# Gathered expert rows in four chains of three half-row cells, and four more mixing-weight units kept on chip

## The chip, the cores and the metric

The kernel runs on one core of one Trainium2 chip. The metric is the device time of one execution, in microseconds (us).

## What is computed

One layer of a hybrid decoder for 1024 prompt tokens and 8 sample tokens, all in float32, D = 1024 channels. A trunk (state-space branch, gated recurrent branch, mixing of the two, output projection) comes first. Behind it stands the expert retrieval, which moves most of the bytes:

```python
q = (xc @ w_q).reshape(PEER_BLOCK, PEER_HEADS, 2, PEER_DK)
...
eidx = jnp.take_along_axis(cidx.reshape(...), sel, axis=-1)      # 8 heads x 16 experts of 16384 for each token
g = jax.nn.softmax(cs, axis=-1)
u = u_tab[eidx]
act = jax.nn.gelu(jnp.einsum('chkd,cd->chk', u, xc).astype(jnp.float32))
w = (g * act).astype(xc.dtype)
return jnp.einsum('chk,chkd->cd', w, v_tab[eidx])
```

So every token needs 128 rows of u (4 KB each) for dot products with its own vector, and the same 128 rows of v (4 KB each), weighted and added. The mixing that the change touches as well is `sigmoid(g_a) * (a_out @ w_proj_a) + sigmoid(g_b) * (b_out @ w_proj_b)`.

## The kernel before

**Chunks and slots.** The prompt is worked on in four chunks (c = 0 to 3) of 256 tokens, two tiles of 128. An expert slot is one expert of each of the 128 tokens of a tile. A chunk has 256 slots, there are 1024 in all and 8 more for the sample tokens. For each slot GpSimd issues one indirect DMA, the gather: it takes 128 rows of the table `uv`, whose rows hold u and v side by side (8 KB), one into each partition, 1 MB together.

**The path of a slot.** The gather lands in one of UV = 8 places of `uvring` (u in the first half of a place, v in the second), in turn. Slot number `at` uses place `at % UV`. VectorE multiplies u by the tokens' vectors and sums (the dot, in `dots`, which signals `u_used`). Two slots make a batch (PAIR = 2): ScalarE turns the two dots into weights (`weigh`) and spreads each on a diagonal `dg`; TensorE multiplies `dg` by v and adds in PSUM (`values`, which signals `v_pe`). A place is free again when TensorE has read v: that is what `gather_to` waits for, eight gathers back. GpSimd does its gathers in order and does nothing else.

**The trunk between the batches.** The trunk of chunk c + 1 is interleaved with the batches of chunk c by hand-written positions (`upto(...)` on each engine): VectorE does the scans, the mixing gates and the top-16 lists in between dots; TensorE the projections in between `values`.

**Weights.** SyncE loads trunk weights through a ring of two 8 KB slots; a pair of units (1 MB for the mixing weights `w_ab`, four pairs) is loaded when the pair two before it has been used. Some units are RESIDENT: loaded once in chunk 0 and kept for chunks 1 to 3. In chunk 0 the eight units of `w_ab` lie in places of the gather ring (from `MIX_AT`) that the first gathers don't need yet, and gathers 4 to 7 wait for the mixing products of chunk 0 (`unit`) before they overwrite them.

Of the kernel before, what the change touches and what calls it, by code (L numbers as in the profile page):

```python
# [14 lines left out]
P = 128  # L15
# [38 lines left out]
UV = 8  # L54
# [26 lines left out]
            ("w_out", 6), ("w_out", 7))  # L81
PARKED = (("w_out", 0),)
GLU_W = tuple(("w_glu", m) for m in range(4))
HOMES = RESIDENT + PARKED + GLU_W + tuple(MIX_W)
# [197 lines left out]

def dve_slots(c, i):

    return max(SLOT * c + i, 0) - pe_slots(c, i)
# [71 lines left out]
def build(nc, i_, o_):  # L357

    with ExitStack() as ctx:
# [6 lines left out]
        def sem(name):  # L366
# [94 lines left out]
        assert W.at <= T.at + UV * 2 * D  # L461
# [3 lines left out]
        uvring = R.take(UV, 2 * D)  # L465
        hn = [R.take(D) for _ in range(2)]
        acc = [R.take(D) for _ in range(2)]
        rows_ = uvring.rearrange("p a b -> p (a b)")
        GLU_AT, MIX_AT = 6 * D, 8 * D
        assert W.at <= T.at + GLU_AT and MIX_AT + KT * D <= UV * 2 * D  # L470
        homes = [R.take(D) for _ in RESIDENT] + [acc[1]] \
            + [rows_[:, GLU_AT + DB * k:GLU_AT + DB * k + DB] for k in range(QT)] \
            + [rows_[:, MIX_AT + D * k:MIX_AT + D * k + D] for k in (LAST_FIRST.index(m) for m in range(KT))]
# [268 lines left out]
        def _(pool):  # L742
# [62 lines left out]
        def _(act):  # L805
# [126 lines left out]
            def first_lists(upto):  # L932
# [42 lines left out]
                square_sum(0, 0, P, uvring[:, 0, 0:D])  # L975
# [232 lines left out]
        def _(dve):  # L1208
# [467 lines left out]
            def last_row():  # L1676
# [3 lines left out]
                return stt(acc[1], uvring[:, place(c, i) % UV, D:2 * D], wt[:, (BC - 1) % DOTS, PAIR - 1:PAIR], acc[1])  # L1680
# [30 lines left out]
            def dots(c, b):  # L1711

                for k in range(PAIR):
# [3 lines left out]
                    u = uvring[:, at % UV, 0:D]  # L1717
# [3 lines left out]
            def row(c, b):  # L1721

                i = PAIR * b + PAIR - 1
                if on_dve(SLOT * c + i) and (c, b) != (CH - 1, BC - 1):
# [3 lines left out]
                    stt(acc[t], uvring[:, place(c, i) % UV, D:2 * D], wt[:, b % DOTS, PAIR - 1:PAIR], acc[t]).then_inc(v_dve, 1)  # L1728
# [42 lines left out]
            def sample():  # L1771

                dve.wait_ge(hnS_in, 16 * NS)
                for h in range(HEADS):
                    at = sample_place(h)
                    dve.wait_ge(uv_in[at % UV], 16 * (at // UV + 1))
                    u = uvring[:, at % UV, 0:D]
# [227 lines left out]
        def _(pe):  # L2005
# [122 lines left out]
            def values(c, b):  # L2128
# [4 lines left out]
                for k in range(PAIR):  # L2133
                    i = PAIR * b + k
                    if not on_dve(SLOT * c + i):
                        last = i - i % (SLOT // 2) + SLOT // 2
                        for half in range(2):
                            at = D + 512 * half
                            for r, o in zip((0, HP), TURNED[half]):
                                ins = mm(PV[o:o + HP, half], dg[r:r + HP, PAIR * (b % 2) + k],  # L2140
                                         uvring[r:r + HP, place(c, i) % UV, at:at + 512],
# [22 lines left out]
            def sample():  # L2164

                for h in range(HEADS):
                    pe.wait_ge(w8_ok, h + 1)
                    for half in range(2):
                        at = D + 512 * half
                        ins = mm(PS[0:NS, half], w8[:, h], uvring[:, sample_place(h) % UV, at:at + 512],  # L2170
# [380 lines left out]
```

## Time and profile before

| what | us |
|---|---|
| median of 3 runs | 3084.43 |
| lowest and highest run | 3083.14, 3085.8 |
| span of the profiled execution | 3084.7 |

The profile gives the execution's span, from its first to its last instruction, and no other time for it; it lies 0.3 us from the median of the runs. In the profile PE is TensorE's matmuls, PEld its weight loads, DVE VectorE, ACT ScalarE, POOL GpSimd, SP SyncE. A line such as L759 is that of a helper, so that one line stands for all gathers (L759), all dots of prompt slots (L1718), all `values` matmuls (L2140), all mixing matmuls (L2184).

### The profile page before, as it was taken

Reading aid. Unit: us, or ns where it says so; the run is one execution under the profiler, and the core shown is the slowest. Engines: PE = TensorE matmul, PEld = TensorE weight load, DVE = VectorE, ACT = ScalarE, POOL = GpSimd, SP = SyncE. Lnnn points to the kernel's source line nnn. Section 1 sums busy time; section 2 is a strip of 40 time slices with the busy share of each in tenths; the row PEclk is TensorE's granted clock in tenths of the full one; section 3 lists DMA queues with packets and bytes.
Section 4 is the critical chain, followed back from the end, with each engine's and each line's share of the span. In section 5 each row is a group of like instructions: output and inputs, shape, how many; then the busy total and the mean of one; then the engine's idle time right before and its main releaser. Section 6 shows DMA issues by size and latency. Waiting matters only on the chain.

```text
span 3084.7 us, 40759 instructions
## 1 busy us (share of the span) xinstructions
PE 2367.6 (77%) x14560; PEld 1190.1 (39%) x14560; DVE 2150.7 (70%) x5361; ACT 1001.2 (32%) x3275; POOL 1202.5 (39%) x1048
## 2 busy tenths in 40 slices
PE   9997769888876778789777678888987676555565
PEld 7864325555343334455233324444433331111111
DVE  7758887765579887665468887766558897544445
ACT  2224332422334332432234332432233443222223
POOL 0013343443344443343343443434344444444442
PEclk9999889999999989989988879999998886777777
DMA  4569999999999999999999999999999999999997
GB/s 154 208 244 398 420 421 420 415 414 399 420 420 418 420 420 419 418 392 420 420 419 417 421 420 408 420 394 420 418 420 420 420 416 419 416 406 420 420 419 328
DMA packets 177898, 1226.32 MB, mean 398 GB/s; under 512 B 22664, under 2 KB 23048, under 8 KB 32160
## 3 DMA queue, kind: packets, MB, share of 16 engines
q0 software_dynamic: 148608, 1082.20, 84.9%
q1 hardware_dynamic: 27440, 136.67, 11.2%
q10 hardware_dynamic: 1648, 4.85, 0.4%
q8 instruction: 115, 1.88, 0.3%
q14 instruction: 87, 0.71, 0.1%
HBM read 1219.09 MB, written 4.55 MB: 397 GB/s over the span
## 4 chain that ended last, share of the span: by engine, by line
DMA 45%; PE 26%; DVE 15%; ACT 5%; POOL 3%; issue 3%; ACTq 1%; DVEq 0%; SPq 0%; POOLq 0%
DMA arena<-in_uv,arena 44%; PE psum L2140 11%; DVE arena L1718 7%; PE psum L2037 7%; ACT arena L807 4%; POOL arena L759 3%; PE psum L2184 3%; DVE arena L1212 3%; PE psum L2204 2%; DVE arena L1220 1%; DMA arena<-in_w_ab 1%; PE psum L2216 1%; ACT L807 1%; ACTq L831 1%; DVE arena L1590 1%
## 5 line engine op out<-in xcount | busy, mean ns | idle before, releaser
L759 POOL DMA_INDIRECT arena<-in_uv,arena x1032 | 1199.3, 1162 | 1856.2 <-PE psum L2140 1525.3
L1718 DVE CUSTOM_DVE_ANT_0 arena<-arena 128x1024 f32<-128x1024 f32 x1024 | 1246.8, 1225 | 789.4 <-DMA arena<-in_uv,arena 781.5
L2140 PE MATMUL psum<-arena 64*64 64x512 f32 x8184 | 1226.7, 723 | 669.9 <-ACT arena L807 622.5
L807 ACT ACTIVATE arena<-arena 128x1 f32<-128x1 f32 (+4 forms) x2746 | 727.1, 302 | 1850.8 <-DVE arena L1718 1741.9
L2140 PEld LDWEIGHTS psum<-arena 64*64 64x64 f32 x8184 | 301.2, 151 | 1401.1 <-ACT arena L807 923.5
L2037 PE MATMUL psum<-arena 128*128 128x256 f32 (+1 forms) x2656 | 632.4, 393 | 7.7 <-ACT arena L807 6.9
L2037 PEld LDWEIGHTS psum<-arena 128*128 128x128 f32 x2656 | 504.3, 194 | 193.6 <-issue 121.8
L1212 DVE TENSOR_TENSOR arena<-arena 128x256 f32<-128x256 f32 (+12 forms) x561 | 249.9, 472 | 12.1 <-issue 0.4
L807 ACT ACT_TABLE_LOAD x119 | 152.7, 1283 | 11.2 <-DVE arena L1212 7.1
L807 ACT ACTIVATE arena<-psum 128x256 f32<-128x256 f32 (+5 forms) x254 | 98.3, 402 | 144.9 <-PE psum L2037 94.4
L2184 PE MATMUL psum<-arena 128*128 128x128 f32 (+2 forms) x640 | 123.6, 351 | 9.5 <-DMA arena<-in_w_ab 7.2
L2184 PEld LDWEIGHTS psum<-arena 128*128 128x128 f32 x640 | 103.2, 196 | 37.2 <-issue 19.4
L1220 DVE SCALAR_TENSOR_TENSOR arena<-arena 128x256 f32<-128x256 f32 (+8 forms) x287 | 99.0, 357 | 19.3 <-ACT arena L807 13.9
L2204 PE MATMUL psum<-arena 128*128 128x512 f32 x192 | 90.3, 614 | 0.0
L1718 DVE DVE_READ_ACCUMULATOR2_ANT arena<- 128x1 f32 x1024 | 83.6, 82 | 0.0
L1486 DVE TENSOR_TENSOR_SCAN arena<-arena 128x64 f32<-128x64 f32 x256 | 68.9, 331 | 1.3
L1220 DVE SCALAR_TENSOR_TENSOR arena<-arena,psum 128x128 f32<-128x128 f32 (+4 forms) x97 | 46.0, 513 | 33.6 <-PE psum L2184 28.9
L2216 PE MATMUL psum<-arena 128*128 128x256 f32 (+1 forms) x320 | 63.2, 354 | 0.4 <-issue 0.4
L1212 DVE TENSOR_TENSOR arena<-psum,arena 128x512 f32<-128x512 f32 (+2 forms) x91 | 59.6, 684 | 2.8 <-PE psum L2140 1.8
L2216 PEld LDWEIGHTS psum<-arena 128*128 128x128 f32 x320 | 52.6, 200 | 22.5 <-issue 17.8
L2204 PEld LDWEIGHTS psum<-arena 128*128 128x128 f32 x192 | 35.2, 193 | 56.3 <-issue 56.3
L2052 PEld LDWEIGHTS psum<-arena 32*128 32x128 f32 x512 | 35.0, 207 | 28.9 <-issue 26.2
(134 smaller groups left out, 981.9 us busy)
## 6 DMA issues: line engine op xcount, KB each, us to landing
arena<-in_w_in SPq DMA_DIRECT2D x56, 1024.0 KB, 9.0
arena<-in_w_q SPq DMA_DIRECT2D x34, 1024.0 KB, 9.4
arena<-in_uv,arena POOLq DMA_INDIRECT x1032, 13.7
arena<-in_w_ab SPq DMA_DIRECT2D x12, 1024.0 KB, 9.4
arena<-in_w_out SPq DMA_DIRECT2D x11, 512.0 KB, 15.8
arena<-in_keys SPq DMA_DIRECT2D x17, 256.0 KB, 8.3
arena<-in_w_ab SPq DMA_DIRECT2D x8, 512.0 KB, 10.8
arena<-in_x_tok SPq DMA_DIRECT2D x8, 512.0 KB
```

Source lines behind the costliest of these rows:

```text
L759: pool.indirect_dma_start(uvring[:, r], None, i_["uv"], bass.IndirectOffsetOnAxis(column, 0)).then_inc(uv_in[r], 16)
L807: return nc.scalar.activation(out, in_, f, **kw)
L1212: return V.tensor_tensor(out, a, b, op)
L1220: return V.scalar_tensor_tensor(out=out, in0=a, scalar=s1, in1=b, op0=op0, op1=op1)
L1486: return V.tensor_tensor_scan(v, mag2[:, j:j + 1].to_broadcast([P, SEG]), v, start, ALU.mult, ALU.add)
L1718: V.tensor_tensor_reduce(out=u, in0=u, in1=hn[i // (SLOT // 2)], scale=1.0, scalar=0.0, op0=ALU.mult, op1=ALU.add, accum_out=dots_[:, b % ...
L2037: ins = mm(PB[u % 2][:, 0:n], w[:, P * t:P * t + P], rhs[:, t, 0:n], start=(t == 0), stop=(t == k - 1))
L2052: ins = mm(SB[j % 2][:, 2 * SEG * part:2 * SEG * part + 2 * SEG], wT[o:o + 32, QT * (2 * r + part) + q], uS[o:o + 32, q, 2 * SEG * r:2 * S ...
L2140: ins = mm(PV[o:o + HP, half], dg[r:r + HP, PAIR * (b % 2) + k], uvring[r:r + HP, place(c, i) % UV, at:at + 512], start=(i % (SLOT // 2) = ...
L2184: ins = mm(banks[side][:, 0:cols.stop - cols.start], w[:, 512 * side + P * t:512 * side + P * t + P], src[:, t, cols], start=(t == 0), sto ...
L2204: ins = mm(OUTB[t][half][0:rn], hT[c][:, k, r0:r0 + rn], w[:, 512 * half:512 * half + 512], start=(k == 0), stop=(k == KT - 1))
L2216: ins = mm(PB[s][:, 0:n], w[:, P * t:P * t + P], gb[:, t, cols], start=(t == 0), stop=(t == KT - 1))
```

## The change

A place now has three 4 KB cells for two slots' worth of turns. There are four chains of three cells; slot `at` belongs to chain `at % 4`. Its u always lands in the middle cell. Its v lands in the left cell on even turns and in the right cell on odd ones, so that u and v are still one 8 KB run in each partition: for the left side a second table `vu` (v first, then u) is gathered. The ring needs 12 cells of 4 KB where it had 8 places of 8 KB. The 16 KB per partition that this frees hold four more units of `w_ab` (2 to 5) for good, so that chunks 1 to 3 load two pairs of `w_ab` where they loaded four. A gather now also waits until the dot of the slot four before it has read the middle cell.

```diff
-UV = 8
+CHAINS = 4
+CELLS = 3 * CHAINS
+UV = 2 * CHAINS
...
 RESIDENT = (("w_out", 1), ("w_out", 2), ("w_out", 3), ("w_out", 4), ("w_out", 5),
-            ("w_out", 6), ("w_out", 7))
+            ("w_out", 6), ("w_out", 7), ("w_ab", 2), ("w_ab", 3), ("w_ab", 4), ("w_ab", 5))
...
-HOMES = RESIDENT + PARKED + GLU_W + tuple(MIX_W)
+MIX_PARKED = tuple(("w_ab", m) for m in LAST_FIRST[0:4])
+MIX_CELLS = (9, 10, 8, 11)
+HOMES = RESIDENT + PARKED + GLU_W + MIX_PARKED
...
+def u_cell(at):
+
+    return 3 * (at % CHAINS) + 1
+
+
+def v_cell(at):
+
+    return 3 * (at % CHAINS) + (2 if at // CHAINS % 2 else 0)
...
-            def gather(r, column):
-                pool.indirect_dma_start(uvring[:, r], None, i_["uv"],
-                                        bass.IndirectOffsetOnAxis(column, 0)).then_inc(uv_in[r], 16)
+            def gather(at, column):
+                first = D * min(u_cell(at), v_cell(at))
+                table = i_["vu"] if v_cell(at) < u_cell(at) else i_["uv"]
+                pool.indirect_dma_start(rows_[:, first:first + 2 * D], None, table,
+                                        bass.IndirectOffsetOnAxis(column, 0)).then_inc(uv_in[at % UV], 16)
 
             def gather_to(at, column):
 
+                before = at - CHAINS
+                if sample_place(0) <= before < sample_place(HEADS):
+                    pool.wait_ge(us_used, before - sample_place(0) + 1)
+                elif before >= 0:
+                    pool.wait_ge(u_used, before - (HEADS if before >= sample_place(HEADS) else 0) + 1)
                 before = at - UV
...
-                gather(at % UV, column)
+                gather(at, column)
...
-                    if c == 0 and i * 2 * D == GLU_AT:
-                        pool.wait_ge(glu_mm, 2 * QT)
-                    if c == 0 and MIX_AT <= i * 2 * D < MIX_AT + KT * D:
-                        m = 2 * i - MIX_AT // D
-                        pool.wait_ge(unit, U_MIX1 + m + 2)
+                    if c == 0 and i < UV:
+                        held = {u_cell(i), v_cell(i)}
+                        if held & {GLU_AT // D, GLU_AT // D + 1}:
+                            pool.wait_ge(glu_mm, 2 * QT)
+                        if held & set(MIX_CELLS):
+                            pool.wait_ge(unit, U_MIX1 + 1 + max(k for k, cell in enumerate(MIX_CELLS) if cell in held))
```

VectorE, TensorE and ScalarE run the same instructions as before, on other addresses.

GpSimd's queue at the start of chunk 0 was this before (`unit` counts finished products of trunk weights, `glu_mm` those of the gate):

```order
L759 DMA arena<-in_uv,arena 128x2048 [waits best_ok]
L759 DMA arena<-in_uv,arena 128x2048 x2
L759 DMA arena<-in_uv,arena 128x2048 [waits glu_mm]
L759 DMA arena<-in_uv,arena 128x2048 [waits unit] x4
L759 DMA arena<-in_uv,arena 128x2048 [waits v_pe,idx_ok]
L759 DMA arena<-in_uv,arena 128x2048 [waits v_pe] x7
```

It is this now:

```order
L775 DMA arena<-in_vu,arena 128x2048 [waits best_ok]
L775 DMA arena<-in_vu,arena 128x2048
L775 DMA arena<-in_vu,arena 128x2048 [waits glu_mm]
L775 DMA arena<-in_vu,arena 128x2048 [waits unit]
L775 DMA arena<-in_uv,arena 128x2048 [waits u_used] x2
L775 DMA arena<-in_uv,arena 128x2048 [waits u_used,unit,glu_mm]
L775 DMA arena<-in_uv,arena 128x2048 [waits u_used,unit]
L775 DMA arena<-in_vu,arena 128x2048 [waits v_pe,u_used,idx_ok]
L775 DMA arena<-in_vu,arena 128x2048 [waits v_pe,u_used] x3
```

From the fifth gather on every gather also waits for a dot (`u_used`), here and to the end of the program.

SyncE's queue at the mixing of chunk 1 was this before:

```order
L634 DMA arena<-in_w_glu 128x1024 [waits unit] x2
L634 DMA arena<-in_w_ab 128x2048 [waits unit] x4
L634 DMA arena<-in_w_out 128x1024 [waits unit]
L661 DMA arena<-in_x_tok 128x1024 [waits y_out0,lru_ok]
L662 DMA arena<-in_x_tok 128x1024
```

It is this now:

```order
L648 DMA arena<-in_w_glu 128x1024 [waits unit] x2
L648 DMA arena<-in_w_ab 128x2048 [waits unit] x2
L648 DMA arena<-in_w_out 128x1024 [waits unit]
L675 DMA arena<-in_x_tok 128x1024 [waits y_out0,lru_ok]
L676 DMA arena<-in_x_tok 128x1024
```

Two loads of 1 MB are gone, and what stands behind them moves up by two turns of the ring. Chunks 2 and 3 read the same.

## Rows read from the trace of the kernel before

**Rows 1.** The page: busy time of the engines, and the 40 slices

```profile
PE 2367.6 (77%) x14560; PEld 1190.1 (39%) x14560; DVE 2150.7 (70%) x5361; ACT 1001.2 (32%) x3275; POOL 1202.5 (39%) x1048
...
DMA  4569999999999999999999999999999999999997
GB/s 154 208 244 398 420 421 420 415 414 399 420 420 418 420 420 419 418 392 420 420 419 417 421 420 408 420 394 420 418 420 420 420 416 419 416 406 420 420 419 328
```

**Rows 2.** The page: the chain that ended last, by engine

```profile
DMA 45%; PE 26%; DVE 15%; ACT 5%; POOL 3%; issue 3%; ACTq 1%; DVEq 0%; SPq 0%; POOLq 0%
```

**Rows 3.** The page's costliest groups: the gather (L759) and the dot (L1718)

```profile
L759 POOL DMA_INDIRECT arena<-in_uv,arena x1032 | 1199.3, 1162 | 1856.2 <-PE psum L2140 1525.3
L1718 DVE CUSTOM_DVE_ANT_0 arena<-arena 128x1024 f32<-128x1024 f32 x1024 | 1246.8, 1225 | 789.4 <-DMA arena<-in_uv,arena 781.5
```

**Rows 4.** Waits: who waited for whom; us in total, times, longest us

```profile
POOL arena L759 <- PE psum L2140: 1525.3, 592, 10.9
...
DVE arena L1718 <- DMA arena<-in_uv,arena: 781.5, 581, 5.2
```

**Rows 5.** Timeline of VectorE: start us, us, instruction, idle before it

```profile
2708.45 1.23 DVE L1718 CUSTOM_DVE_ANT_0 arena<-arena 128x1024 f32<-128x1024 f32 x1 [1.26 <-DMA arena<-in_uv,arena]
...
2710.93 1.23 DVE L1718 CUSTOM_DVE_ANT_0 arena<-arena 128x1024 f32<-128x1024 f32 x1 [1.25 <-DMA arena<-in_uv,arena]
```

**Rows 6.** The gather's line alone: ns min/median/max, and us to landing

```profile
L759 POOL DMA_INDIRECT arena<-in_uv,arena x1032: 932/940/2665, 188.7 to 3057.9; - x172
...
DMA to landing us min/median/max: 5.5/13.7/21.8
```

**Rows 7.** The same view of the one gather issued at 749.0

```profile
DMA to landing us min/median/max: 6.8/6.8/6.8
```

**Rows 8.** The page's DMA issues: mixing weights; count, KB each, us to landing

```profile
arena<-in_w_ab SPq DMA_DIRECT2D x12, 1024.0 KB, 9.4
```

**Rows 9.** Windows over mixing stages; last three numbers: clock, DMA share, GB/s

```profile
736.00:746.00 10.00, 10.00 (x61) 7.62 (x60) 2.83 (x8) 0.95 (x4) 1.87 (x2) 0.99 1.02 392
746.00:762.00 16.00, 16.00 (x95) 9.88 (x94) 13.19 (x25) 3.82 (x15) 7.27 (x5) 1.00 0.91 339
...
1411.00:1460.00 49.00, 47.09 (x272) 30.35 (x271) 26.98 (x53) 10.49 (x40) 17.37 (x16) 0.97 1.01 420
2138.00:2185.00 47.00, 44.06 (x261) 27.27 (x260) 27.32 (x57) 10.25 (x38) 15.67 (x15) 1.00 1.01 421
```

**Rows 10.** The chain at the mixing of chunk 1: start us, us, what

```profile
719.53 10.69 DMA arena<-in_w_ab
...
740.78 6.91 PE psum L2184 x32
...
778.83 18.11 DMA arena<-in_uv,arena
```

**Rows 11.** Timeline of VectorE early in chunk 0

```profile
232.47 1.22 DVE L1718 CUSTOM_DVE_ANT_0 arena<-arena 128x1024 f32<-128x1024 f32 x1
...
242.57 1.23 DVE L1718 CUSTOM_DVE_ANT_0 arena<-arena 128x1024 f32<-128x1024 f32 x1 [1.23 <-DMA arena<-in_uv,arena]
...
252.53 0.87 DVE L1545 MAX8 arena<-arena 128x8 f32<-128x128 f32 x4 [8.73 <-ACTq L949]
...
256.31 1.21 DVE L1718 CUSTOM_DVE_ANT_0 arena<-arena 128x1024 f32<-128x1024 f32 x1
```

**Rows 12.** Timeline of GpSimd there

```profile
225.61 0.94 POOL L759 DMA_INDIRECT arena<-in_uv,arena  x1 [0.30 <-issue]
```

**Rows 13.** The gather's line again: the one issued at 1832.2

```profile
L759 POOL DMA_INDIRECT arena<-in_uv,arena x1: 1481/1481/1481, 1832.2 to 1832.2; - x1
...
DMA to landing us min/median/max: 12.8/12.8/12.8
```

**Rows 14.** Timeline of VectorE behind it

```profile
1850.98 1.23 DVE L1718 CUSTOM_DVE_ANT_0 arena<-arena 128x1024 f32<-128x1024 f32 x1
...
1859.97 1.23 DVE L1718 CUSTOM_DVE_ANT_0 arena<-arena 128x1024 f32<-128x1024 f32 x1 [3.17 <-DMA arena<-in_uv,arena]
```

More of the change, by code:

```diff
@@ L460, in build @@
         big, big2 = W.take(HJ, SEG), W.take(HJ, SEG)
-        assert W.at <= T.at + UV * 2 * D
+        assert W.at <= T.at + CELLS * D
         R = Arena(arena, T.at)
-        uvring = R.take(UV, 2 * D)
+        cells = R.take(CELLS, D)
         hn = [R.take(D) for _ in range(2)]
         acc = [R.take(D) for _ in range(2)]
-        rows_ = uvring.rearrange("p a b -> p (a b)")
-        GLU_AT, MIX_AT = 6 * D, 8 * D
-        assert W.at <= T.at + GLU_AT and MIX_AT + KT * D <= UV * 2 * D
+        rows_ = cells.rearrange("p a b -> p (a b)")
+        GLU_AT = 6 * D
+        assert W.at <= T.at + GLU_AT and min(MIX_CELLS) * D >= GLU_AT + QT * DB
         homes = [R.take(D) for _ in RESIDENT] + [acc[1]] \
             + [rows_[:, GLU_AT + DB * k:GLU_AT + DB * k + DB] for k in range(QT)] \
-            + [rows_[:, MIX_AT + D * k:MIX_AT + D * k + D] for k in (LAST_FIRST.index(m) for m in range(KT))]
+            + [cells[:, k] for k in MIX_CELLS]
         dg = R.take(2 * PAIR, HP)
@@ L974, in first_lists @@
                 act.sem_inc(tr_ev, 1)
-                square_sum(0, 0, P, uvring[:, 0, 0:D])
+                square_sum(0, 0, P, cells[:, 0])
                 act.sem_inc(sq2_ok, 1)
@@ L1679, in last_row @@
                 dve.wait_ge(w_ok, dve_slots(c, i) + 1)
-                return stt(acc[1], uvring[:, place(c, i) % UV, D:2 * D], wt[:, (BC - 1) % DOTS, PAIR - 1:PAIR], acc[1])
+                return stt(acc[1], cells[:, v_cell(place(c, i))], wt[:, (BC - 1) % DOTS, PAIR - 1:PAIR], acc[1])
             def add_sums(c, t):
@@ L1716, in dots @@
                     dve.wait_ge(uv_in[at % UV], 16 * (at // UV + 1))
-                    u = uvring[:, at % UV, 0:D]
+                    u = cells[:, u_cell(at)]
                     V.tensor_tensor_reduce(out=u, in0=u, in1=hn[i // (SLOT // 2)], scale=1.0, scalar=0.0, op0=ALU.mult,
@@ L1727, in row @@
                     dve.wait_ge(w_ok, dve_slots(c, i) + 1)
-                    stt(acc[t], uvring[:, place(c, i) % UV, D:2 * D], wt[:, b % DOTS, PAIR - 1:PAIR], acc[t]).then_inc(v_dve, 1)
+                    stt(acc[t], cells[:, v_cell(place(c, i))], wt[:, b % DOTS, PAIR - 1:PAIR], acc[t]).then_inc(v_dve, 1)
             def batches(c, lo, hi, prev):
@@ L1776, in sample @@
                     dve.wait_ge(uv_in[at % UV], 16 * (at // UV + 1))
-                    u = uvring[:, at % UV, 0:D]
+                    u = cells[:, u_cell(at)]
                     V.tensor_tensor_reduce(out=u, in0=u, in1=hn[0], scale=1.0, scalar=0.0, op0=ALU.mult,
@@ L2137, in values @@
                         for half in range(2):
-                            at = D + 512 * half
+                            at = 512 * half
                             for r, o in zip((0, HP), TURNED[half]):
                                 ins = mm(PV[o:o + HP, half], dg[r:r + HP, PAIR * (b % 2) + k],
-                                         uvring[r:r + HP, place(c, i) % UV, at:at + 512],
+                                         cells[r:r + HP, v_cell(place(c, i)), at:at + 512],
                                          start=(i % (SLOT // 2) == 0), stop=(pe_slots(c, i + 1) == pe_slots(c, last)))
@@ L2168, in sample @@
                     for half in range(2):
-                        at = D + 512 * half
-                        ins = mm(PS[0:NS, half], w8[:, h], uvring[:, sample_place(h) % UV, at:at + 512],
+                        at = 512 * half
+                        ins = mm(PS[0:NS, half], w8[:, h], cells[:, v_cell(sample_place(h)), at:at + 512],
                                  start=(h == 0), stop=(h == HEADS - 1))
@@ L2527 @@
         "uv": np.concatenate([a["peer_u"][0], a["peer_v"][0]], axis=1),
+        "vu": np.concatenate([a["peer_v"][0], a["peer_u"][0]], axis=1),
         "nffnT": chans(a["norm_ffn"][0]), "nfinT": chans(a["norm_final"]), "norm_final": a["norm_final"],
```

## The prediction

> **What bounds the kernel now.** I read the page first. No engine is busy all the time (TensorE 77%, VectorE 70%), but the line of the DMA engines shows 9 in nearly every slice from the fourth on, and the bytes stand at about 420 GB/s [rows 1]. The chain that ended last runs through transfers for 45% of the span [rows 2]. Among the groups the dot (L1718) has 789 us of idle time ahead of it, nearly all of it until a gather lands [rows 3]; it waited so 581 times, which leaves some 440 of the 1024 dots of prompt slots that found their row there already and came late themselves [rows 3, 4]. In VectorE's timeline the dots stand 2.48 us apart where they wait, each of them 1.23 us long [rows 5]. So 2.48 us is what 1 MB costs on the DMA engines, and where a dot waits, only bytes, or an empty DMA queue, move the end.
>
> GpSimd is idle for 1525 us until TensorE frees a place [rows 4]. That wait costs nothing while enough gathers are in the queue: the median gather lands 13.7 us after its issue, and the fastest after 5.5 [rows 6]. The difference, 8.2 us, is time in the queue, more than three gathers' worth.
>
> **What the change saves.** Of the 12 loads of 1 MB of mixing weights [rows 8] six go. At 2.48 us each that is 14.9 us of DMA time. The other six, and the eight of 0.5 MB in chunk 0, stay as they are. What each removed load is worth depends on its stage [rows 9]. At the mixing of chunks 2 and 3 the DMA engines move 420 and 421 GB/s, all they can: four loads, 9.9 us saved. At the mixing of chunk 1 they move 392 GB/s for 10 us and 339 GB/s for 16 us; against 421 that is 29/421 x 10 + 82/421 x 16 = 3.8 us in which they lack work. There the chain runs through TensorE's mixing matmuls from 730 us, and gathers come back into it only at 778.8 [rows 10]. So the 5.0 us of these two loads go mostly into a queue that is empty anyway. I take 0 for them, with 5.0 as the other end.
>
> **What the new wait costs.** A gather may now be issued only when the dot of four slots before is done. GpSimd's issues are in order, so a gather that waits for a dot holds all later ones, and the dots behind them wait in turn. Where dots wait for gathers, such a gather lands at the earliest 1.23 (the dot) + 0.30 (from release to issue, the gap that stands ahead of an issue [rows 12]) + 5.5 = 7.0 us after the start of the dot four back. It is due 4 x 2.48 = 9.9 us after it. The cover is 2.9 us. A gather in the queue then waits about 8.4 us from issue to landing instead of 13.7, and GpSimd's idle time is ended by the dot instead of by TensorE. That alone costs nothing. It is gone where a dot comes more than 2.9 us late because VectorE does trunk work. In the old ring the place was released by TensorE's reading of v, eight slots back, which left up to five or six gathers in the queue.
>
> So each late stretch has to be priced. Start of chunk 0: VectorE makes dots 8 to 13 in one run from 232.47 [rows 11], but gather 13 was issued at 225.61 [rows 12]. Now gathers 12 to 15 follow dots 8 to 11: issues at 234.0, 235.2, 236.4 and 237.5. The first lands at 239.5 and the last, three spacings on, at 247.0, where dot 15 ran at 242.57. These 4.4 us disappear, since VectorE's next step stood idle for 8.73 us, until 252.53 [rows 11]. Behind it dots resume at 256.31, and gathers 20 and up now need dot 16, so the first of them lands 257.5 + 0.3 + 5.5 = 263.3. The DMA engines have done about 2 gathers less by then. Part of that is made up where VectorE comes late itself. The ends are 0 (all of it made up) and 8 (the 4.4 us, and 1.5 gathers' spacing more), and I take 4 between them.
>
> Chunk 3's trunk gives the clearest late place: the gather issued at 1832.2 had landed at 1845.0 [rows 13], its dot ran at 1850.98 [rows 14], 5.9 us late. That is 5.9 - 2.9 = 3.0 us of empty queue, and the dot at 1859.97 waited for a transfer before as well [rows 14], so VectorE has no slack to take it. I price this place at 3.0. Most of the 440 late dots are the second of a pair or follow a short piece of trunk work, and are less than 2.9 us late; for the few places of 3 to 5 us that I expect among the rest I add 2, a choice. Together 5, with 0 (every late place followed by other slack) and 12 (four such places) as ends. The dry stretch in chunk 1's mixing belongs here too: gathers come later there as well, 0 to 3 us, counted 0 with the two loads.
>
> An issue costs GpSimd 0.94 us in the median, and up to 2.67 [rows 6]. Issues now start right behind a dot, often beside the next one. I take 1 us in all for that, 0 to 5 as ends. The Trainium skill, SBUF — State Buffer, "Who interferes with whom", says that a VectorE instruction with two SBUF inputs contends with a GpSimd instruction that reads SBUF, the later one being blocked. By it an issue beside a dot could take a dot's length more, which would cut the cover from 2.9 to about 1.7 us; the median of 0.94 says that most issues are not held so.
>
> The wait for v, the three-cell layout and the second table add no byte and no instruction; packets stay 8 KB. I count them at nothing. GpSimd's own queue: one more semaphore wait for each gather is hidden by its 1525 us of idle time. SyncE's queue: the output weights and token rows behind the removed loads move up by one or two ring turns, into the same stretch, at nothing.
>
> The shortest landing, 5.5 us, is of an empty queue. The gather issued at 749.0 took 6.8 us [rows 7]; with that the cover is 1.6 us. The Trainium skill, DMA: Bandwidth & Descriptors, "Anatomy of one DMA", gives 2.0 us plus bytes over 436 GB/s; an estimate by it is 4.4 us for 1 MB and a cover of 4.0. The rows decide; I stay at 5.5.
>
> **Sum.** -9.9 (chunks 2 and 3) + 0 (chunk 1) + 4 (start) + 5 (late places) + 1 (issues) = +0.1 us. The profiled span is 3084.7 and the median 3084.43; I give 3084.5.
>
> **The rivals.**
> *Only bytes count.* If late dots are always followed by idle time of VectorE that takes the delay, as behind dot 15, the loss is near 0 and chunk 1 gives part of its two loads: -9.9 - 2 + 2 = -10, 3074 us; at best -14.9, 3069.5. For it speaks that the first delay is swallowed whole [rows 11]; against it, that at 1859.97 VectorE waited for transfers already. 24%.
> *The queue runs dry.* The other side. The real cover is the 1.6 us of [rows 7], so more of the 440 late dots count. Start 8 + late places 12 + issues 1 = 21, less 9.9: +11, 3095.5 us. It decides once the losses pass 9.9 + 6.2 = 16 us. For it speaks that VectorE is late at over four in ten of its dots. 19%.
> *GpSimd is held by VectorE.* Each issue beside a dot takes up to 1.2 us more. The cover is 1.7 us and the late places cost about as much as in the rival above, with the issue's mean well over the 1162 ns of [rows 3]: 3092 to 3098. The skill's rule on the shared port stands behind it. 6%.
> That the change doesn't remove the loads is excluded by SyncE's order.
>
> **How the numbers follow.** Runs of this kernel differ by 2.7 us; 0.2%, 6.2 us, is about what a measurement can tell from no change. The forecast, within 6.2 us of 3084.4, has 51%. Faster by more is the first rival, 24%; slower the other two, 25%. The range leaves out a tenth on either side: 3076 (most of the bytes, small losses) to 3095 (a dry queue).
>
> **What would show it.** Six fewer 1 MB loads of `w_ab`. The median gather lands after about 8 to 9 us instead of 13.7, and GpSimd's idle time is ended mostly by the dot. In the windows of the mixing of chunks 2 and 3 the rate is still 415 or more; if it is under 410 there, the cover is too small. The rate dips more between 225 and 270 us, near 745 and near 1856, and nowhere else by much. The tail behind the last gather is unchanged. The prediction is wrong if the rate in the last 450 us falls (dots there are never late), if the packets of the two tables take longer, or if VectorE's idle time swallows all delays.

## The result, and the profile after

The changed kernel takes 3157.85 us in the median of 4 runs (3146.34 to 3166.57), the kernel before 3085.11 in the same session: a ratio of 1.0234 [1.0219, 1.0248]. It is 72.7 us slower, and 62.9 us above the upper end of my range.

The page of the changed kernel (busy time, slices, chain), which answers to [rows 1, 2]:

```profile
PE 2379.3 (75%) x14560; PEld 1195.0 (38%) x14560; DVE 2157.7 (68%) x5361; ACT 1000.8 (32%) x3275; POOL 1103.8 (35%) x1048
...
DMA  4559999999999999999999999999999999999998
GB/s 150 220 218 394 383 390 406 400 418 381 412 415 376 395 395 416 409 404 410 420 406 388 386 390 389 397 405 413 410 413 408 378 397 402 416 407 420 420 420 356
...
DMA 31%; issue 23%; PE 21%; POOL 10%; DVE 9%; ACT 3%; ACTq 1%; DVEq 0%; POOLq 0%; SPq 0%
```

The busy line of the DMA engines shows 9 as before, and hides the loss. The rate under it shows it: where the kernel before had 415 to 421 GB/s in most slices, there are 376 to 418 in most, everywhere but in the last ones. In the chain of waits, transfers fell from 45% to 31%, and "issue" with GpSimd took 33% in place of 6%: the path now runs from a dot through an issue to a landing.

Its groups (the gather is now L775, two tables; the dot is L1740) and its waits, for [rows 3, 4]:

```profile
L1740 DVE CUSTOM_DVE_ANT_0 arena<-arena 128x1024 f32<-128x1024 f32 x1024 | 1248.2, 1224 | 875.6 <-DMA arena<-in_vu,arena 447.6
...
L775 POOL DMA_INDIRECT arena<-in_vu,arena x516 | 554.9, 1075 | 1085.9 <-DVE arena L1740 652.3
L775 POOL DMA_INDIRECT arena<-in_uv,arena x516 | 545.8, 1058 | 952.3 <-DVE arena L1740 800.3
```

```profile
POOL arena L775 <- DVE arena L1740: 1452.6, 695, 10.6
...
DVE arena L1740 <- DMA arena<-in_vu,arena: 447.6, 320, 4.3
...
DVE arena L1740 <- DMA arena<-in_uv,arena: 418.3, 309, 5.0
POOL arena L775 <- PE psum L2162: 322.5, 172, 5.4
```

GpSimd waits 695 times for a dot and only 172 times for TensorE. The dots wait 84 us more in all for rows than before. The loads went as the edit says, 6 of 1 MB left:

```profile
arena<-in_w_ab SPq DMA_DIRECT2D x6, 1024.0 KB, 10.4
```

Windows over the mixing of chunk 2, of chunk 3 and of chunk 1 (both stretches of [rows 9], as long behind the start of its matmuls), then a trunk stretch with its mixing (gathers 128 to 256) and the tail (gathers 896 to 1031). Behind the bounds stand the length, the busy time of TensorE's matmuls, its weight loads, VectorE, ScalarE and GpSimd, then the clock, the DMA share and GB/s:

```profile
1458.00:1507.00 49.00, 47.08 (x278) 28.96 (x277) 27.03 (x52) 10.55 (x41) 14.76 (x16) 0.97 1.01 409
2208.00:2255.00 47.00, 45.00 (x258) 27.86 (x257) 27.43 (x56) 10.93 (x42) 16.93 (x15) 0.96 1.01 405
758.00:768.00 10.00, 10.00 (x61) 7.59 (x60) 3.12 (x10) 1.27 (x5) 0.94 (x1) 0.99 0.81 316
768.00:784.00 16.00, 16.00 (x96) 9.88 (x94) 11.32 (x22) 3.80 (x15) 7.39 (x6) 1.00 0.78 289
...
586.00:968.00 382.00, 322.26 (x1924) 176.27 (x1924) 251.15 (x596) 125.38 (x408) 137.02 (x130) 0.93 0.99 405
2807.00:3150.00 343.00, 195.71 (x1068) 46.27 (x1072) 172.32 (x280) 94.03 (x350) 126.12 (x133) 0.78 1.01 415
```

The same two stretches of work in the kernel before:

```profile
566.00:942.00 376.00, 317.47 (x1928) 175.62 (x1924) 249.79 (x596) 125.59 (x408) 151.22 (x129) 0.94 1.01 413
2728.00:3072.00 344.00, 202.28 (x1068) 47.20 (x1072) 172.81 (x280) 94.06 (x350) 153.18 (x131) 0.75 1.00 410
```

The prediction set 410 GB/s in the mixing of chunks 2 and 3 as the sign of a cover that is too small: they show 409 and 405. The tail takes 343 us against 344, so nothing is lost where VectorE has little but dots to do. Everything is lost ahead of it: by landings, the changed kernel is 20.6 us behind at gather 128, 25.7 at gather 256, 79.0 at gather 896 and 78.5 at the last one.

### The profile page after: what moved, and what is told of

It reads as the page before. It is cut to its first block, busy times and chain, and to the rows that moved or that the text cites. A ratio compares the mean times of both kernels' runs of the same rounds, so it can differ in the third digit from the quotient of the medians.

```text
span 3161.7 us, 41745 instructions
## 1 busy us (share of the span) xinstructions
PE 2379.3 (75%) x14560; PEld 1195.0 (38%) x14560; DVE 2157.7 (68%) x5361; ACT 1000.8 (32%) x3275; POOL 1103.8 (35%) x1048
## 4 chain that ended last, share of the span: by engine, by line
DMA 31%; issue 23%; PE 21%; POOL 10%; DVE 9%; ACT 3%; ACTq 1%; DVEq 0%; POOLq 0%; SPq 0%
DMA arena<-in_vu,arena 19%; DMA arena<-in_uv,arena 12%; POOL arena L775 10%; PE psum L2162 9%; PE psum L2059 5%; DVE arena L1740 5%; ACT arena L829 3%; PE psum L2206 3%; DVE arena L1234 2%; PE psum L2226 1%; DMA arena<-in_w_ab 1%; DVE arena L1242 1%; PE psum L2238 1%; PE psum L2273 0%; ACTq L853 0%
## 5 line engine op out<-in xcount | busy, mean ns | idle before, releaser
L1740 DVE CUSTOM_DVE_ANT_0 arena<-arena 128x1024 f32<-128x1024 f32 x1024 | 1248.2, 1224 | 875.6 <-DMA arena<-in_vu,arena 447.6
L775 POOL DMA_INDIRECT arena<-in_vu,arena x516 | 554.9, 1075 | 1085.9 <-DVE arena L1740 652.3
L775 POOL DMA_INDIRECT arena<-in_uv,arena x516 | 545.8, 1058 | 952.3 <-DVE arena L1740 800.3
L1740 DVE DVE_READ_ACCUMULATOR2_ANT arena<- 128x1 f32 x1024 | 83.9, 82 | 0.0
```

Source lines behind the costliest of these rows:

```text
L775: pool.indirect_dma_start(rows_[:, first:first + 2 * D], None, table, bass.IndirectOffsetOnAxis(column, 0)).then_inc(uv_in[at % UV], 16)
L1740: V.tensor_tensor_reduce(out=u, in0=u, in1=hn[i // (SLOT // 2)], scale=1.0, scalar=0.0, op0=ALU.mult, op1=ALU.add, accum_out=dots_[:, b % ...
```

## The experiments

All times are medians, with the ratio to the kernel before measured in the same session (3084.6 to 3085.6 us).

| run | us | ratio [95%] |
|---|---|---|
| lead4: wait for the dot four back | 3166.41 | 1.0262 [1.0244, 1.0279] |
| lead5: five back | 3093.28 | 1.0028 [1.0018, 1.0039] |
| lead6: six back | 3084.96 | 0.9996 [0.9987, 1.0006] |
| swap_sides: two tables | 3085.69 | 1.0001 [0.9991, 1.001] |
| fewer: loads alone | 3068.82 | 0.9946 [0.9932, 0.9959] |
| both: loads and wait | 3159.83 | 1.0234 [1.0218, 1.025] |
| tail4: wait in the tail only | 3084.25 | 0.9998 [0.9989, 1.0007] |
| hold4: lead4, issues 0.5 us later | 3214.03 | 1.042 [1.0403, 1.0436] |
| hold0: the same without the wait | 3084.8 | 0.9998 [0.9989, 1.0008] |
| short4: lead4, dots of 512 columns | 3093.23 | 1.0027 [1.0018, 1.0036] |
| short0: the same without the wait | 3083.67 | 0.9993 [0.9984, 1.0002] |
| reduce4: lead4, sums in place of dots | 3132.39 | 1.0156 [1.014, 1.0173] |
| reduce0: the same without the wait | 3076.86 | 0.9975 [0.9965, 0.9985] |
| later4: lead4, with drains on GpSimd | 7398.98 | 2.3992 [2.3955, 2.4029] |
| later0: drains alone | 7410.86 | 2.4025 [2.3988, 2.4061] |
| ring7: seven places, two blocks kept | 3094.54 | 1.0027 [1.0018, 1.0036] |
| chains5: five chains, one block kept | 3087.38 | 1.0007 [0.9998, 1.0016] |

**Which part costs: the wait or the layout.** Four kernels, each the kernel before with one thing added. The wait alone (LEAD is 4, 5 or 6), ahead of the old one:

```
+                before = at - LEAD
+                if sample_place(0) <= before < sample_place(HEADS):
+                    pool.wait_ge(us_used, before - sample_place(0) + 1)
+                elif before >= 0:
+                    pool.wait_ge(u_used, before - (HEADS if before >= sample_place(HEADS) else 0) + 1)
                 before = at - UV
```

> The kernel before with its eight whole places and its one table, and only the new wait added: a gather also waits for the dot four slots back. All mixing weights are loaded as before. Theory 1 (the wait empties the transfer queue): the change lost 73 us although it moves six loads fewer, worth up to 14.9 us, so this kernel takes 3150 to 3180 us and its median gather lands after 8 to 9 us. Theory 2 (the layout: u and v change sides, two tables, and each packet takes longer): 3095 to 3100 us, which is what the prediction's own prices give for the wait alone.

> As the one before, but the wait is for the dot five slots back. Theory 1: one more gather of 2.48 us in the queue; if the cover is what counts, most of the loss goes, 3090 to 3110 us. If a constant cost of waiting on the dot at each issue is to blame (the wait's own handling on GpSimd, or an issue beside a dot), about as slow as with four back. Theory 2: within 5 us of 3085.

> The wait is for the dot six slots back. Theory 1: within 6 us of 3085, as six slots back is where TensorE's release already stands. A constant cost of the wait: as slow as with four or five back. Theory 2: 3085.

And the two tables alone, in the old ring with the old wait:

```
+                table = i_["uv"] if u_half(at) == 0 else i_["vu"]
-                pool.indirect_dma_start(uvring[:, r], None, i_["uv"],
+                pool.indirect_dma_start(uvring[:, at % UV], None, table,
```

> The kernel before with eight places of 8 KB and no new wait, but u and v change sides within a place every four slots, gathered from the table and from a second one with v ahead of u. Theory 1: same as before, 3085 within 3 us. Theory 2: 3140 to 3175 us, and over 2% of the 8 KB packets take longer than 0.4 us.

The wait four back costs 81.6 us without any other part of the change, five back 8.5, six back nothing, the two tables nothing. The slices of the rate with the dot five back (first fence) and four back (second):

```profile
GB/s 154 207 245 383 409 417 420 419 411 420 415 420 404 417 420 420 420 395 420 420 419 410 410 419 411 419 411 420 419 418 418 415 411 418 420 407 421 419 421 338
```

```profile
GB/s 150 223 215 401 392 401 411 410 405 378 412 415 374 399 385 405 407 399 419 420 417 386 386 393 399 413 400 415 419 408 404 391 390 396 415 405 419 421 421 350
```

**What the loads are worth.** The saved loads in the old ring, then together with the wait. Other weights stand in for those that aren't loaded, so these two compute something else:

```
+STANDIN = (("w_ab", 2), ("w_ab", 3), ("w_ab", 4), ("w_ab", 5))
...
+    if c and weight(c, l) in STANDIN:
+        return STANDIN.index(weight(c, l))
```

> The kernel before with the old ring and no new wait, but in chunks 1 to 3 the mixing blocks 2 to 5 of w_ab are not loaded: their products read the output blocks that lie on the chip as stand-ins, so the mixed rows of chunks 1 to 3 are computed with other weights. It measures the six saved loads of 1 MB alone. My forecast (loads of chunks 2 and 3 worth 2.48 us each, those of chunk 1 nothing) gives -9.9: about 3075. If chunk 1's loads are worth their bytes as well, -14.9: 3070. From the two kernels measured so far (the wait alone 3166.4, the whole change 3157.9) the loads give back about 8.6 in the changed kernel. If the loads were worth nothing, 3085.

> The old ring with the wait for the dot four slots back, and without loads of the mixing blocks 2 to 5 in chunks 1 to 3 (stand-ins, so chunks 1 to 3 are computed with other weights). It is the changed kernel without the three-cell layout and the early homes. If the two effects add (the wait +81.6, the loads -16.6): 3150, and the 8 us up to the changed kernel's 3158 belong to the layout or to the homes in chunk 0. If a saved load is worth less where the queue runs dry: 3155 to 3160, and the layout costs nothing here either.

Alone the six loads give 16.6 us. Beside the wait they give 81.6 - 74.5 = 7.1 us (6.6 by the medians as they stand). The intervals of the two runs are about 5 us wide to either side, so this can be anything from 0 to 14, but hardly 16.6. So the two effects don't add: where the queue runs dry, a saved byte bought less. The kernel with both parts in the old ring stands where the changed kernel does (1.0234 both). The three-cell layout and the early homes cost nothing that can be measured, which here means nothing above some 6 us.

**Where dots come on time.** One line decides where the wait is four back:

```
-                before = at - LEAD
+                before = at - (4 if at >= 896 else UV)
```

> The kernel before with the wait for the dot four slots back for the last 136 gathers alone, where VectorE has little but dots to do. Theory A (only late dots lose, a dot on time is 0.3 us within the limit): 3084 to 3087. Theory B (fewer gathers in the queue move fewer bytes wherever they are): 136 of 1032 gathers' share of 82 us is 10.8, 3096.

Nothing is lost: gathers 896 to 1031 land within 343.0 us, where they took 343.9 in the kernel before. Each lands 8.4 us after its issue there, 3.4 spacings. So three to four gathers on their way are enough to keep the DMA engines full, if they come on time.

**Issues later, or earlier.** To push each issue back I first put writes with a drain behind each ahead of the gather:

```
+                for _ in range(3):
+                    pool.iota(spare, [[1, 1]], base=0, channel_multiplier=0, allow_small_or_imprecise_dtypes=True)
+                    pool.drain()
                 gather(at % UV, column)
```

> The wait for the dot four slots back in the kernel before (3166.4), and between the wait and each gather three writes of one element with a drain behind each on GpSimd: some 0.4 to 0.8 us between the release and the issue. Theory A (a gather needs about 5.5 us between its issue and the landing of the gather ahead; on-time dots give 5.8): now even gathers whose dots come on time are issued too late, by 5.2 us ahead or less. Each then loses about 0.1 us (a loss lets the next one be issued relatively earlier), some 70 to 100 us over the gathers that dots wait for, and the late ones 20 to 40 more: 3230 to 3320, and the rate falls in the tail as well, where it did not before. By my prediction's cover of 2.9 us only late dots count, and the delay adds 0.6 us to each of the few: 3170 to 3200, with the tail untouched.

> The kernel before with the same small writes and drains on GpSimd ahead of each gather, without the new wait. GpSimd is idle for 1525 us in the kernel before, and gathers are issued 9 us or more ahead of the landing before them: no change, 3080 to 3095. All theories agree here; it shows what the delay costs by itself.

This pair misses its purpose: both take 2.4 times as long, with or without the wait, since the first drain behind a gather lasts until that gather has landed (the one issued at 1208.15 lands at 1213.75). GpSimd's timeline of the run without the wait:

```profile
1208.15 0.95 POOL L760 DMA_INDIRECT arena<-in_uv,arena  x1 [0.77 <-issue]
1209.10 0.15 POOL L775 IOTA arena<- 128x1 f32 x1
1213.90 0.39 POOL L775 IOTA arena<- 128x1 f32 x2 [4.65 <-issue]
1215.06 0.96 POOL L760 DMA_INDIRECT arena<-in_uv,arena  x1 [0.77 <-issue]
```

The pair is of use for something else. In the run without the wait 1031 gathers are issued when the one before has landed, and so show what an empty queue costs. They land 5.5 us after their issue in the median, as the fastest ones of the kernel before did. By the packets' records the first packet starts 0.70 us after the issue's end. The packets then take 3.55 us from the first start to the last end, where 2.48 is a gather's share of a full queue: the first 16 last 0.78 us each in the median, those of the second half 0.31. The landing is signalled 0.34 us behind the last packet.

The second try has a semaphore in place of the drain:

```
+                for n in range(3):
+                    if at or n:
+                        pool.wait_ge(spare_ok, 3 * at + n)
+                    pool.iota(spare, [[1, 1]], base=0, channel_multiplier=0,
+                              allow_small_or_imprecise_dtypes=True).then_inc(spare_ok, 1)
```

> As the run with writes and drains on GpSimd, but without the drain, which held each gather until the one before had landed: the wait for the dot four slots back in the kernel before (3166.4), and between the wait and each gather three writes of one element, each waiting for a semaphore of the one before: some 0.4 to 0.8 us. Theory A (a gather needs about 5.5 us between its issue and the landing of the gather ahead; a dot on time gives 5.8): now gathers whose dots come on time are too late as well, 3230 to 3320, and the last 136 gathers, which took 343 us with and without the wait, take 350 to 370. By a cover of 2.9 us only late dots count: 3170 to 3200, and the last 136 stay at 343.

> The kernel before with the same three writes ahead of each gather and no new wait. Gathers are issued 9 us or more ahead of the landing before them, and GpSimd is idle for 1525 us: 3080 to 3090 by all theories.

The writes take 0.53 us, then 0.15 to the issue. From the end of the dot to the issue it is 0.76 us in place of 0.28, so each issue comes half a microsecond later. GpSimd's timeline of the run with the wait, in the tail, and the gather's line over 100 us of it:

```profile
2906.49 0.53 POOL L784 IOTA arena<- 128x1 f32 x3 [0.85 <-DVE arena L1731]
2907.17 0.95 POOL L762 DMA_INDIRECT arena<-in_uv,arena  x1 [0.15 <-POOL arena L784]
```

```profile
L762 POOL DMA_INDIRECT arena<-in_uv,arena x40: 946/952/963, 2899.7 to 2997.9; - x40
...
DMA to landing us min/median/max: 7.7/7.9/9.1
```

With the wait in the tail only, without the writes, the same line reads:

```profile
L760 POOL DMA_INDIRECT arena<-in_uv,arena x40: 939/939/954, 2861.3 to 2959.3; - x40
...
DMA to landing us min/median/max: 8.1/8.4/9.2
```

Half a microsecond costs 47.6 us over the wait alone, under the 64 that I had set as the least. Between landings 896 and 1031 the tail takes 347.0 us in place of 343.0: dots on time begin to lose as well, 0.03 us a gather. So the cover of an on-time dot is not 2.9 us, or the tail would have stayed at 343. Nearly all of the 47.6 us, however, is lost ahead of the tail, where dots come late as well.

The other way, dots over half the columns (the scores are wrong then):

```
-                    V.tensor_tensor_reduce(out=u, in0=u, in1=hn[i // (SLOT // 2)],
+                    V.tensor_tensor_reduce(out=u[:, 0:512], in0=u[:, 0:512], in1=hn[i // (SLOT // 2)][:, 0:512],
```

> The wait for the dot four slots back in the kernel before (3166.4), with dots over 512 of the 1024 columns, so that each takes about 0.6 us less; scores and so the weights of the rows differ from the reference. Compare with the same short dots without the wait. Theory A (a gather must be issued about 5.5 us ahead of the landing of the gather before it; with the wait four back a dot on time gives 5.8, so anything over 0.3 to 1 us late is lost): 0.6 us more room, and fewer late dots, take the loss from 82 to 20 to 40 us. Theory B (with only three gathers in the queue the DMA engines themselves move less, whatever the dots do): the loss stays at 65 to 85. My prediction's cover of 2.9 us would make it under 10, as it would have made the first.

> The kernel before with dots over 512 of the 1024 columns and no new wait: the base for the run with both. VectorE does 640 us less; if bytes bound nearly everywhere, 0 to 20 us less than before: 3065 to 3085. All theories agree here.

The loss falls from 81.6 to 3093.2 - 3083.7 = 9.5 us, where my theory of late dots had 20 to 40. This run changes several things at once: the release comes 0.6 us earlier, a shorter dot can hold an issue for less time, and VectorE is late less often. Without the wait 154 dots start more than 0.8 us behind their landing, in place of 269. So it doesn't say which of them gave the most.

**An issue that a dot holds.** The timelines of the changed kernel show it. VectorE, from the end of a list's work at 1907.4, then GpSimd:

```profile
1907.41 1.23 DVE L1740 CUSTOM_DVE_ANT_0 arena<-arena 128x1024 f32<-128x1024 f32 x1
...
1908.57 1.22 DVE L1740 CUSTOM_DVE_ANT_0 arena<-arena 128x1024 f32<-128x1024 f32 x1
...
1910.86 1.29 DVE L1740 CUSTOM_DVE_ANT_0 arena<-arena 128x1024 f32<-128x1024 f32 x1
...
1917.13 1.23 DVE L1740 CUSTOM_DVE_ANT_0 arena<-arena 128x1024 f32<-128x1024 f32 x1 [4.97 <-DMA arena<-in_uv,arena]
```

```profile
1908.92 1.67 POOL L775 DMA_INDIRECT arena<-in_uv,arena  x1 [6.70 <-DVE arena L1740]
1910.89 0.94 POOL L775 DMA_INDIRECT arena<-in_uv,arena  x1 [0.30 <-issue]
```

The first late dot ends at 1908.6 and releases the gather; the next dot has begun at 1908.57 and ends at 1909.79. The issue starts at 1908.92 and lasts 1.67 us, to 0.80 us after that dot's end, where one by itself lasts 0.94. It stood still while the dot ran. Its rows land at about 1917.1, and VectorE is idle for 4.97 us. In the trace of the wait alone, 148 issues begin beside a running dot and take longer than 1.1 us, 114 us in all over 0.94, and in the median they end 0.81 us behind that dot.

The same trace shows what holds an issue in an instruction of VectorE. VectorE's TENSOR_TENSOR over 512 columns lasts 0.68 us with both inputs in SBUF (`arena`) and with one of them in PSUM, and writes to SBUF either way. Two issues that begin in the second of a pair of them, at 1219.47 and at 1175.60:

```profile
1218.80 1.29 DVE L1218 TENSOR_TENSOR arena<-arena 128x512 f32<-128x512 f32 x2
1219.47 1.43 POOL L760 DMA_INDIRECT arena<-in_uv,arena  x1 [2.50 <-DVE arena L1724]
...
1174.93 1.28 DVE L1218 TENSOR_TENSOR arena<-psum,arena 128x512 f32<-128x512 f32 x2
1175.60 0.94 POOL L760 DMA_INDIRECT arena<-in_uv,arena  x1 [2.76 <-DVE arena L1724]
```

All 37 issues that began over 0.22 us ahead of the end of one with both inputs in SBUF took 1.14 us or more; the 19 beside one with an input in PSUM took 0.94. So there it is the second input from SBUF, and neither the length nor the write; the dot reads two as well.

In that trace I worked out for each gather from the 20th on how long ahead of the landing of the gather before it its issue ended, and how much longer than 2.48 us (and the time of other bytes at 421 GB/s) its own landing came behind that one:

| issue ended ahead of that landing, us | gathers | lost each, us | in all |
|---|---|---|---|
| under 3 | 61 | 0.75 | 45.7 |
| 3 to 4 | 48 | 0.58 | 27.7 |
| 4 to 4.5 | 66 | 0.12 | 7.9 |
| 4.5 to 5 | 314 | 0.03 | 8.6 |
| over 5 | 523 | 0.07 | 38.7 |

The last rows are a floor: the kernel before, where nearly all gathers have over 6 us, shows about 47 us by the same measure. The step is at 4 us: 109 gathers below it lose 73 us. In the kernel before there are 6 such gathers.

To part the hold from the lateness, each dot became a sum of the same length with one operand (wrong scores again):

```
-                    V.tensor_tensor_reduce(out=u, in0=u, in1=hn[i // (SLOT // 2)], scale=1.0, scalar=0.0, op0=ALU.mult,
-                                           op1=ALU.add, accum_out=dots_[:, b % DOTS, k:k + 1]).then_inc(u_used, 1)
+                    V.reduce_sum(dots_[:, b % DOTS, k:k + 1], u, AX).then_inc(u_used, 1)
```

> The wait for the dot four slots back in the kernel before (3166.4), with each dot replaced by a plain sum over the same 1024 columns of u, so the scores are wrong; a sum over 1024 columns takes about 1.22 us in these traces, as the dot does, but reads one operand in place of two. In the trace with the wait, 143 issues that begin while a dot runs take about 1.7 us in place of 0.94, since they stand until the dot ends; those beside a sum or a search take 0.94. Theory C (the loss comes for the larger part from issues held by the dot of the next slot: late dots come in pairs, the first one's end releases the issue and the second one's run holds it): the issues take 0.94, and the loss against the same sums without the wait falls from 82 to 15 to 35 us, about 3110. Theory A (late dots alone, with a small cover, whatever the issue takes): 70 to 90 stay, 3160. By a limit counted from the end of the issue (109 gathers whose issue ended under 4 us ahead of the landing of the gather before lost 73 of the 82 us), C is the likelier.

> The kernel before with each dot replaced by a plain sum over the 1024 columns of u, without the new wait: the base for the run with both. VectorE's time stays, issues take 0.94 in place of 1.16 us in the mean, and gathers have room enough anyway: 3078 to 3088 by all theories.

The groups of this kernel with the wait, VectorE's sum and GpSimd's gather, and then the gather's group with dots and the same wait:

```profile
L1724 DVE TENSOR_REDUCE arena<-arena 128x1 f32<-128x1024 f32 x1024 | 1240.1, 1216 | 859.0 <-DMA arena<-in_uv,arena 843.4 <-issue 7.2
...
L760 POOL DMA_INDIRECT arena<-in_uv,arena x1032 | 997.7, 967 | 2106.9 <-DVE arena L1724 1484.5 <-PE psum L2145 367.2 <-DVEq L1661 184.9
```

```profile
L760 POOL DMA_INDIRECT arena<-in_uv,arena x1032 | 1101.7, 1068 | 2045.0 <-DVE arena L1724 1409.3 <-PE psum L2146 355.9 <-DVEq L1661 185.1
```

The sum is as long as the dot (1216 and 1224 ns), the issue 967 ns in place of 1068. The loss is 3132.4 - 3076.9 = 55.5 us in place of 81.6. So about a third, 26 us, was the hold by dots, and two thirds the lateness, with what holds are left beside other instructions. By the measure of the table 103 gathers of this kernel have under 4 us and lose 50 us; only 19 of them have under 3, where 61 had. Neither theory's range has it: I had expected 15 to 35 of one and 70 to 90 of the other.

**Versions that could have beaten both.** Seven places in the old ring, and blocks 4 and 5 of `w_ab` kept:

```
-UV = 8
+UV = 7
...
+            ("w_out", 6), ("w_out", 7), ("w_ab", 4), ("w_ab", 5))
```

> A version that could beat both: the ring of places of before, released by TensorE's reading of v as before, with seven places in place of eight; the 8 KB freed keep blocks 4 and 5 of w_ab on the chip, so three loads of 1 MB are saved (7.4 us at 2.48). A gather now waits for v seven slots back. If a gather needs only about 5.5 us between its issue and the landing of the gather ahead of it, the old ring has room for this nearly everywhere (the wait for the dot six back cost nothing and five back 8.5): loss 0 to 8, 3077 to 3086, 3080 the likeliest. If every place less costs as the step from five to four dots back did, the loss is tens of us: 3110 or more.

And the changed kernel with a fifth chain:

```
-CHAINS = 4
+CHAINS = 5
...
-            ("w_out", 6), ("w_out", 7), ("w_ab", 2), ("w_ab", 3), ("w_ab", 4), ("w_ab", 5))
+            ("w_out", 6), ("w_out", 7), ("w_ab", 5))
```

> The changed kernel with five chains of three cells (ten places) in place of four: a gather waits for the dot five slots back, and one mixing block stays on the chip (block 5, so that three pairs of w_ab load as 0.5 MB in place of 1 MB: 3.7 us at 1.24 each). The wait for the dot five back alone cost 8.5 us; less 3.7 at most: 3087 to 3093, 3090 the likeliest. If the layout hides a cost that shows only together with the wait, it lies above 3095.

Neither beats the kernel before. Seven places cost more than the three loads give, 9.1 us net. Five chains are within measurement of it, at 3087.4. The wait five back cost 8.5 us alone, and 1.8 is left of it; three loads cut to half give 3.7 by their bytes. Where the other 3 us came from wasn't parted.

## Why the prediction was wrong

**What bounds the kernel** held. The dot waits for rows, 2.48 us is the spacing, and the saved loads alone are worth more than I said: 16.6 us, where bytes at 2.48 give 14.9. The term for chunk 1, taken as 0 of its 5.0 us, was too small: between the landings of gathers 128 and 256 the kernel without the loads takes 373.3 us in place of 376.4, so some 3 of the 5.0 came. That is one trace each; three other traces of kernels that do the same there have 375.5 to 378.1.

**The step that failed is "The cover is 2.9 us."** I set it as 9.9 less 7.0, where 7.0 had the shortest landing, 5.5 us, in it. That landing is of a gather that finds an empty queue, when the DMA engines already stand idle. To keep them busy the gather must be ready before the queue is empty, and before the first of the 16 engines is done, not the last. In the trace of the changed kernel, first and last signal the end of their part of a gather 2.1 us apart in the median. On an empty queue a gather lands 4.59 us after the end of its issue, 2.1 us more than its 2.48: 0.70 until the first packet, 1.07 by which the packets take longer than 2.48, and 0.34 behind the last. The two make 4.2 us, and the table's step is at 4. That sum is argued; the step, and the loss that follows when issues move by half a microsecond, are measured. With dots on time an issue ends 4.99 us ahead in the median of the tail, so the real cover is about 1.0 us for an issue by itself. The terms that rested on 2.9 were 4 + 5 + 1 = 10 us for the wait; it cost 81.6.

The loss is not only idle time of the DMA engines. Between the profiled executions of the kernel before and of the wait alone lie 85.9 us. The 16 engines are idle for 33.9 us more each, and the packets of the gathers, 8 KB as before, last 52.1 us more for each engine: 2844 of them take over 0.45 us in place of 816. In the changed kernel, around the held issue of 1908.92:

```profile
1909.00:1916.00 7.00, 4.71 (x36) 2.18 (x40) 3.16 (x6) 3.21 (x14) 4.41 (x4) 0.76 0.95 353
```

The share is 0.95 at 353 GB/s, since long packets count as busy. That is why the line of the DMA engines showed 9 throughout. Why packets behind a late issue last longer isn't shown.

**The late places were the other half of it.** I priced one place that I saw at 3.0 us, added 2 by choice, and said that most of the 440 late dots were under 2.9 us late. Most were, but not enough of them. Landing and dot paired over the whole trace of before, 63 dots came more than 2.9 us late; counting each run of late dots once, by its worst, they exceed 2.9 us by 40 us in all, and 1.0 us by about 115 us. Part of it is made up again, and lead4 measured 81.6 us. So even with the cover of 2.9 the count was short. My 5, with 12 as the upper end, came from one place when the trace held them all.

**The rival "GpSimd is held by VectorE"** had 6% and is true in part. I set it aside on the median issue of 0.94 us [rows 6]. But the issues that matter are those behind late dots, and there the next dot runs already. The mean of an issue even fell, from 1162 ns [rows 3] to 1067, while the held ones moved onto the path. The Trainium skill, SBUF — State Buffer, "Who interferes with whom", says that a VectorE instruction with two SBUF inputs contends with a GpSimd instruction that reads SBUF. The runs agree: 1.67 us beside the dot, 1.43 beside a TENSOR_TENSOR with both inputs in SBUF, and no hold beside the one-input sum or with one input in PSUM. The 33 issues of over 1.3 us that are left beside a TENSOR_TENSOR in the kernel with sums fit it as well. An issue held to 1.67 us has about 0.3 us left of the cover of 1.0. In price it was 26 of 82 us, not a case by itself.

**The rival "The queue runs dry"** was the right mechanism at 19%, with a price of 21 us where 82 were measured: its cover of 1.6 us was still above the real one of about 1.0, and its late places, 12 us, were still counted from one place.

**The start of chunk 0**, priced 4 with 8 as the end, was delayed as described: gather 15 lands at 249.2 where I had 247.0. But more follows. At the landing of gather 20, 265.4 in place of 261.2, the kernel is 4.2 us behind; at gather 128, 586.3 in place of 565.7, it is 20.6 us behind. That stretch has late dots all along, and my sum for it stopped at gather 20.

**Signs.** Most came as forecast: six loads gone, gathers landing after 8.8 us in the median, GpSimd released by the dot, the tail untouched, no cost of the two tables. The two that failed are the rates in the mixing, 409 and 405 in place of 415 or more, and the dips, which were not confined to three places.

**Still open.** Sums in place of dots make even the kernel without the wait 7.7 us faster (3076.9). They don't write u back, and hold no issue; which of the two it is wasn't tried. Why five back still costs 8.5 us was not parted either.

## What to carry to other kernels

A ring's cover is not the slack to the shortest landing seen. It is the slack to the moment from which the queue begins to lose, and that is better read as how long ahead of the landing before it each transfer is issued; here it had to be 4 to 4.5 us from the end of the issue. A DMA line that shows 9 doesn't exclude the loss, the rate under it does. When a wait is moved to an engine that has other work, pair every release with its consumer over the whole trace and sum the lateness at two or three covers; one late place is no sample. And look at what the releasing engine does next: if it starts an instruction that holds the issuing engine, the release comes later by that instruction's length.

## What the runs showed of the hardware

- A gather of 1 MB loses no more than the floor (0.03 to 0.08 us) when its issue ends 4.5 us or more ahead of the landing of the one before it, and 0.6 to 0.75 us when it ends under 4 us ahead. With each landing 8.4 us after its issue the tail takes 343.0 us, as with more on their way (343.9).
- A gather on an empty queue lands 5.5 us after its issue: the first packet starts 0.70 us after the issue's end, and the first 16 packets last 0.78 us each in place of 0.31.
- An issue of a gather on GpSimd that begins while VectorE runs a dot stands until the dot ends: 1.67 us in place of 0.94. With a sum over one operand in its place the mean is 967 ns. Beside a TENSOR_TENSOR of 512 columns it takes up to 1.43 us with both inputs in SBUF and 0.94 with one in PSUM.
- A drain on GpSimd behind a gather lasts until the gather has landed: 4.65 us idle at 1213.90, and 7411 us in all in place of 3085.
- The same six loads were worth 16.6 us with a full queue and about 7 us (0 to 14 by the intervals) with one that runs dry.
